# Expert outputs scattered to DRAM rows and gathered by token, in place of a matrix product that combines them

## The reference

```python
grp_p = softmax(t @ router_grp + router_grp_b)        # 4 groups, the best one is taken
exp_logits = (t @ router_exp + router_exp_b)          # 8 experts in that group, the top 2 are taken
# weights w1, w2 of the two experts of each token
y[token] = w1 * expert(e1, t[token]) + w2 * expert(e2, t[token])
expert(e, t) = (silu(t @ w_gate[e]) * (t @ w_up[e])) @ w_down[e]   # 1024 -> 256 -> 1024
x = x + gate * y
out = rmsnorm(x, final_norm_g)
```

## Time and profile before

| | |
|---|---|
| median of 3 runs | 2294.93 us (2294.24 to 2294.96) |
| the profiled execution: its own time, its span | 2294.58 us, 2292.7 us |
| loop over the experts (first L2770 to the last L2868) | 1982.66 to 2273.8 us |
| from there to the end of the span | 18.9 us |
| PE busy over the span | 2112.8 us, 92% |
| mean of the DMA engines in 1993 to 2240 us | 0.87 busy, 360 GB/s |

### The profile page before, as it was taken

The page is one execution under the profiler, slowest core; times in us unless marked ns, Lnnn a source line. Parts: engine busy times, 40 slices in busy tenths (PEclk is TensorE's granted clock), DMA queues, the critical chain, the costliest instruction groups (busy, mean ns, idle before and its releaser), DMA issues. The chain is left out here.

```text
span 2292.7 us, 36330 instructions
## 1 busy us (share of the span) xinstructions
PE 2112.8 (92%) x15874; PEld 1296.2 (57%) x15874; DVE 798.8 (35%) x1625; ACT 512.7 (22%) x1042; POOL 101.1 (4%) x103
## 2 busy tenths in 40 slices
PE   6989999999999999999998887899988997799996
PEld 3545568854445658864544776885488643333332
DVE  1474323211185323310245446436344413311112
ACT  2223322201114413210121332123331201211111
POOL 0000000000000000000000011000012000000000
PEclk9999999999999999999998988899999998899998
DMA  6351325533343236334211000100110163298881
GB/s 260 146 201 56 145 110 220 221 147 147 127 187 139 104 124 257 147 147 155 92 43 51 3 3 2 48 13 37 74 40 3 45 258 131 97 391 349 351 347 59
DMA packets 30507, 313.87 MB, mean 137 GB/s; under 512 B 4744, under 2 KB 7184, under 8 KB 9488
## 3 DMA queue, kind: packets, MB, share of 16 engines
q1 hardware_dynamic: 28048, 308.40, 34.3%
q0 software_dynamic: 2304, 3.15, 0.4%
HBM read 330.39 MB, written 3.16 MB: 145 GB/s over the span
## 5 line engine op out<-in xcount | busy, mean ns | idle before, releaser
L511 ACT ACTIVATE arena<-pair 128x512 f32<-128x512 f32 (+5 forms) x339 | 181.0, 547 | 698.7 <-PE pair L885 170.6
L1262 PE MATMUL pair<-arena,weight_ring 128*128 128x256 f32 x1408 | 310.5, 383 | 2.9 <-ACT arena L785 2.9
L885 PE MATMUL pair<-weight_ring,arena 128*128 128x512 f32 (+1 forms) x640 | 277.0, 586 | 19.1 <-issue 11.3
L1262 PEld LDWEIGHTS pair<-arena,weight_ring 128*128 128x128 f32 x1408 | 269.7, 192 | 43.7 <-issue 6.8
L885 PEld LDWEIGHTS pair<-weight_ring,arena 128*128 128x128 f32 x640 | 122.9, 195 | 155.6 <-issue 150.1
L1308 PE MATMUL pair<-weight_ring,arena 128*128 128x512 f32 x352 | 151.5, 592 | 3.1 <-DVE arena L1282 3.1
L1282 DVE SCALAR_TENSOR_TENSOR arena<-pair,columns,arena 128x255 f32<-128x255 f32 (+1 forms) x176 | 76.7, 477 | 201.8 <-ACT arena L1273 200.3
L1308 PEld LDWEIGHTS pair<-weight_ring,arena 128*128 128x128 f32 x352 | 66.8, 190 | 86.7 <-issue 83.2
L1568 PEld LDWEIGHTS pair<-arena 64*64 64x64 f32 x3584 | 111.9, 140 | 4.4 <-issue 3.7
L1568 PE MATMUL pair<-arena 64*64 64x64 f32 x3584 | 113.8, 224 | 0.0
L1382 PE MATMUL pair<-weight_ring,arena 128*128 128x512 f32 (+1 forms) x256 | 106.5, 574 | 4.5 <-DVE arena L704 4.5
(11 more groups left out here) (473 smaller groups left out, 2642.1 us busy)
## 6 DMA issues: line engine op xcount, KB each, us to landing
weight_ring<-stream SPq DMA_DIRECT2D x85, 2048.0 KB, 7.4
weight_ring<-experts_in SPq DMA_DIRECT2D x17, 2048.0 KB, 10.3
arena<-experts_in SPq DMA_DIRECT2D x15, 2048.0 KB, 11.6
arena<-experts_out SPq DMA_DIRECT2D x8, 2048.0 KB, 14.3
weight_ring<-experts_out SPq DMA_DIRECT2D x8, 2048.0 KB, 13.2
weight_ring<-stream SPq DMA_DIRECT2D x4, 1024.0 KB, 4.8
arena<-rows_in SPq DMA_DIRECT2D x1, 3264.0 KB, 21.8
weight_ring<-stream SPq DMA_DIRECT2D x2, 1152.0 KB, 5.1
```

The lines of the kernel that those rows point to most:

```text
L511: copy_act = lambda dst, src: nc.scalar.activation(dst, src, ACT_F.Copy)
L885: last = mm(bank[b][:, 0:n], hT[:, k, m * P:(m + 1) * P], w[:, k * n:k * n + n], start=(j == 0), stop=(j == KD - 1))
L1262: last = mm(bank[b][:, j * S:(j + 1) * S], w[:, at:at + P], hT[:, k, :], start=(k == 0), stop=(k == KD - 1))
```

## The change

The sorted outputs of the experts are written to a DRAM tensor `y_dram` with a row of 4 KB for each of the 512 places and 16 spare rows. For each pair GpSimd issues one indirect store of `Y`'s 128 rows, 64 for each expert of the pair. A row past the end of its expert goes to a spare row if it is in one of the first 16 partitions, and is left out otherwise. After the last pair four indirect loads fetch, for each of the two halves of the tokens and each of their two choices, 128 rows of 4 KB, and DVE adds them to `x` with their weight. `combine`, `combine_weights`, `posT`, `wT` and their spreading go. `Y` is now scaled by the gate row as DVE reads it from PSUM (both halves on DVE), and the outputs' banks alternate between 2, 3 and 4, 5. The last norm is done for each half of the tokens by itself, with two stores, and the table for the root is loaded ahead. The overflow pairs stand at positions 5, 9, 13 and 17.

```diff
-            for at, w in ((3, 32), (8, 34), (13, 36), (18, 38)):
+            for at, w in ((5, 32), (9, 34), (13, 36), (17, 38)):
...
-            for b, values, out_ in ((0, slots2, posT), (1, w12, wT)):
-                take(b)
...
-            spread_done = c.act
+            def sorted_rows():
+
+                link(tt(picked, taken_by, by_slot(ends), ALU.mult))
+                link(nc.vector.tensor_reduce(limits[:, N_EXP:N_EXP + 8], picked, AX, ALU.add))
+                nc.vector.tensor_copy(limits[:, 0:N_EXP], ends)
+                nc.vector.tensor_scalar(row_at[0:CH], firsts[0:CH, 0:40:2], k3c("slot", 1)[0:CH], None, ALU.add)
+                nc.vector.tensor_scalar(row_spare, k3c("slot", 1), k3c("skip", 1), 2.0 * S, ALU.subtract, ALU.add)
+                link(nc.vector.tensor_scalar(row_at[CH:P], firsts[CH:P, 1:40:2], k3c("slot", 1)[CH:P], -float(CH),
+                                             ALU.add, ALU.add))
+                tt(row_ok[0:CH], row_at[0:CH], limits[0:CH, 0:40:2], ALU.is_lt)
+                link(tt(row_ok[CH:P], row_at[CH:P], limits[CH:P, 1:40:2], ALU.is_lt))
+                link(nc.vector.scalar_tensor_tensor(row_at, row_at, row_spare, row_ok, ALU.subtract, ALU.mult))
+                link(nc.vector.tensor_scalar(row_at, row_at, row_spare, None, ALU.add))
+                nc.vector.tensor_copy(places_i[:, 0:20], row_at)
+                return nc.vector.tensor_copy(places_i[:, 20:24], place2.rearrange("p c m -> p (c m)"))
+            places_mark = dve_after(sorted_rows, ("dve", c.dve))
...
-            def combine_weights(i):
...
             def expert_outputs(i):
-                hT, Y = hTs[i % 2], Ys[i % 2]
+                hT, Y, ob = hTs[i % 2], Ys[i % 2], 2 + 2 * (i % 2)
...
-                    if i >= 1:
-                        PE.wait_ge(act_done, left_done[i - 1])
-                        PE.wait_ge(dve_done, right_done[i - 1])
+                    if i >= 2:
+                        PE.wait_ge(dve_done, rows_done[i - 2])
...
-                    nc.scalar.activation(Y[:, 0, :], bank[2][:, :], ACT_F.Copy).then_inc(act_done, 1)
...
-                    nc.vector.tensor_copy(Y[:, 1, :], bank[3][:, :]).then_inc(dve_done, 1)
+                        DVE.wait_ge(y_sent, 16 * (i - 1))
+                    for h_ in range(2):
+                        last = tt(Y[:, h_, :], bank[ob + h_][:, :], grow[:, 1, 512 * h_:512 * h_ + 512], ALU.mult)
...
-            def combine(i):
...
+            def rows_out(i):
+
+                at = pair_windows[i] // 2
+                if POOL:
+                    POOL.wait_ge(dve_done, rows_done[i])
+                    if i:
+                        POOL.wait_ge(y_sent, 16 * i)
+                    POOL.indirect_dma_start(out=y_dram, out_offset=bass.IndirectOffsetOnAxis(ap=places_i[:, at:at + 1], axis=0),
+                                            in_=Ys[i % 2].rearrange("p a b -> p (a b)"), in_offset=None,
+                                            bounds_check=2 * S + 15, oob_is_err=False).then_inc(y_sent, 16)
...
+            for i in range(npairs + 1):
                 if i < npairs:
                     expert_inputs(i)
                 if 1 <= i < npairs - 1:
                     open_window(i + 1)
                 if 1 <= i <= npairs:
                     hidden(i - 1)
-                if i >= 2:
-                    combine(i - 2)
-                if i < npairs:
-                    combine_weights(i)
                 if 1 <= i <= npairs:
                     expert_outputs(i - 1)
+                    rows_out(i - 1)
...
+            if POOL:
+                POOL.wait_ge(act_done, window_copied[npairs - 1])
+                POOL.wait_ge(dve_done, places_mark[1])
+                POOL.wait_ge(y_sent, 16 * npairs)
+                for m in range(TT):
+                    for q in range(2):
+                        POOL.indirect_dma_start(
+                            out=back[2 * m + q], out_offset=None, in_=y_dram,
+                            in_offset=bass.IndirectOffsetOnAxis(ap=places_i[:, 20 + 2 * q + m:21 + 2 * q + m], axis=0),
+                            bounds_check=2 * S - 1, oob_is_err=False).then_inc(y_back[2 * m + q], 16)
+
+            root_ready = act_after(lambda: nc.scalar.activation(ss[:, 32:33], ss[:, 32:33], ACT_F.Sqrt), ("act", c.act))
+            def last_rows(m):
...
+                def add_experts():
+                    for q in range(2):
+                        if DVE:
+                            DVE.wait_ge(y_back[2 * m + q], 16)
+                        last = nc.vector.scalar_tensor_tensor(x[:, m, :], back[2 * m + q], w12[:, q, m:m + 1], x[:, m, :],
+                                                              ALU.mult, ALU.add)
...
+            together([last_rows(m) for m in range(TT)], [])
```

More of the change, by code:

```diff
@@ L240, in build @@
         stored = sem("stores_done")
+        y_sent = sem("sorted_rows_out")
+        y_back = [sem(f"sorted_rows_back{i}") for i in range(4)]
         spilled = sem("u_spilled")
@@ L2895, in program @@
-            norm_rows(x[:, :, :], xn, TT)
-            for m in range(TT):
-                dve_step(lambda: tt(xn[:, m, :], xn[:, m, :], tail("fin", D), ALU.mult))
+                    rows_out(i - 1)
+            back = [sorted_x.rearrange("p a b -> p (a b)")[:, D * q:D * q + D] for q in range(4)]
+            if POOL:
[8 more added lines that the diff above has]
+                            bounds_check=2 * S - 1, oob_is_err=False).then_inc(y_back[2 * m + q], 16)
@@ new lines, in program, with squares, scaled @@
+            root_ready = act_after(lambda: nc.scalar.activation(ss[:, 32:33], ss[:, 32:33], ACT_F.Sqrt), ("act", c.act))
+            def last_rows(m):
+                s1 = ss[:, m:m + 1]
+                def add_experts():
[4 more added lines that the diff above has]
+                                                              ALU.mult, ALU.add)
+                        if q == 0:
+                            link(last)
+                    return last
+                m_x = dve_after(add_experts)
+                yield
+                def squares():
+                    link(nc.scalar.activation(xn[:, m, :], x[:, m, :], ACT_F.Square, accum_out=s1))
+                    return copy_act(xn[:, m, 0:1], xn[:, m, 0:1])
+                a = act_after(squares, m_x, root_ready)
+                yield
+                d = dve_after(lambda: nc.vector.tensor_scalar(s1, s1, 1.0 / D, EPS, ALU.mult, ALU.add), a)
+                a = act_after(lambda: nc.scalar.activation(s1, s1, ACT_F.Sqrt), d)
+                yield
+                def scaled():
+                    link(nc.vector.reciprocal(s1, s1))
+                    return nc.vector.scalar_tensor_tensor(xn[:, m, :], x[:, m, :], s1, tail("fin", D), ALU.mult, ALU.mult)
+                d = dve_after(scaled, a)
+                if SP:
+                    SP.wait_ge(done[d[0]], d[1])
+                    SP.dma_start(out.rearrange("b (m p) d -> p (b m) d", p=P)[:, m, :], xn[:, m, :]).then_inc(stored, 16)
+                yield
```

68 lines of the change are left out of this document (11 added, 57 removed).

## The result

19 runs of the changed kernel have a median of 2303.34 us (2293.35 to 2313.81), 19 runs of the kernel before on the same chip 2295.79 us. The ratio is 1.0037, with a 95% interval of 1.0025 to 1.0048: slower by 0.37%, 8.5 us (the two medians are 7.6 us apart), where 7.7 us less were forecast. The profiled execution took 2301.17 us with a span of 2299.2, against 2294.58 and 2292.7. The lines of the code have moved: inputs L2777 (before L2770), transposes L2804, copy L2812, outputs L2829, scalings L2841, scatter L2853, gather L2876, additions L2890.

What follows compares the result with a forecast made beforehand. PE bound the kernel, loads close behind and setting the pace after the change. Start and loop 2.7, last pair 4.6 and end 0.4 us saved gave a span of 2285.0, forecast 2287.2 us; own range 2281 to 2291, 8-in-10 range 2276 to 2301.

Steps and rivals of the forecast that it cites:

- the first wait: At pair 3, now plain: five loads must land first, at 2017.9 us, so PE waits 4.9 us.
- the end: After the last scalings: last scatter, four gathers, additions, norm and stores, 22.3 us against 22.7 before.
- The rival of slow trips at the end: Scatter and gather at the end each take 7.5 us, 6.2 us more; chance 0.23 jointly with costlier scatters in the loop.
- From pair 3 to pair 19: 16 loop steps: four overflow pairs at 24.9 us per two steps, eight other steps at 15.27 us, from 2017.9 to 2239.7.
- signs of being wrong: Waitless step far from 11.4 us, plain steps over 16, PE clock under 0.9 in the loop, or end over 26.
- Double step, 24.9: From the start of the pair before an overflow pair to that of the pair behind: 24.9 us, against 28.5 before.
- Plain step, 14.77 without scatter: In runs of plain pairs three 2 MB loads at 426 GB/s set the step: 14.77 us, plus the scatter's share.
- The scatter's share, 0.5 us: Each indirect store in the loop adds 0.5 us to a plain step; bounds 0 and 2 us.
- overflow loads at nothing: The small overflow loads fit in the dry stretch of the load queue around an overflow pair, at no cost.
- The clock: PE's clock drops after waits of about 4 us in the loop; one drop of 3.5 us counted, bounds 0 and 21.
- The rival, which needed four and a half drops to decide: Clock drops before each overflow pair and in the first and last pairs: six, 17.5 us more, 2304.7 us; chance 0.2.
- The rival of uneven scatter: Scatter rows on few DMA engines add 2 us to loads, 12 us over 8 steps; chance 0.23 jointly with slow end trips.

Runs made afterwards that it cites:

- e5: The changed kernel run again, unaltered; ratio 1.0041 to the kernel before.
- e13: The changed kernel with only the last pair's scatter, one row in place of 16 in overflow loads and at most one spare row; ratio 0.9997 to the kernel before.
- e1: The changed kernel with two idle products before the inputs of each plain pair from pair 3 on; 2310.90 us, ratio 1.0053 to the kernel before.
- e6: The changed kernel with the 16 rows of an overflow load spread over every fourth partition; ratio 1.0026 to the kernel before.
- e9: The changed kernel with four slots for input weights and three for output weights, input loads first; 2286.13 us, ratio 0.9954 to the kernel before.
- e11: The kernel before with only the slots dealt out anew, four for input and three for output weights; ratio 1.0008 to the kernel before.
- e10: The changed kernel with four input and three output slots, one row in overflow loads and at most one spare row; 2274.52 us, ratio 0.9885 to the kernel before.
- e8: The changed kernel with all 128 rows of every scatter written, unused ones to spare rows; ratio 1.0095 to the kernel before.

## Why the prediction was wrong

Right were: that the loads take over from PE; PE's step (11.43 for 11.37); the start (1981.56 for 1981.65); the first wait (2018.4 for 2017.9); the last pair (12.2 for 12.5); the end (23.3 for 22.3, its two DRAM trips included); no wait at an overflow pair. The rival of slow trips at the end falls: the scatter landed after 2.6 us, the gathers after 4.2 to 6.2. Scatters took 966 to 1218 ns of POOL, but none of the 20 ran while VectorE was busy. Eight other indirect DMAs did, seven overflow loads and a gather, for 0.07 to 0.96 us each, and took 987 to 1001 ns, no more than the others of their kind (993 to 1039). So nothing is to be seen here of the lock in the Trainium skill, "SBUF — State Buffer", section "A bandwidth-pool intuition that's wrong (but worth ruling out)"; its example is a copy on VectorE, and here VectorE ran `tensor_tensor` and `scalar_tensor_tensor`.

**The step that failed is "From pair 3 to pair 19".** 221.8 us were forecast for it, plus 3.5 for the clock; the two profiles have 238.3 and 232.8, so 13.0 and 7.5 us more, and that is the whole miss: with 0.5 at the start, -0.3 in the last pair and 1.0 at the end, 13.0 makes the 14.2 by which the span is over its forecast of 2285.0. In the second profile (e5) the span is 2304.0: there the loop also starts 9.4 us later than forecast, which is no effect of the change, since nothing ahead of it is altered and the four profiles of the kernel before and its variants start it between 1982.5 and 1990.1 as well. Of the signs of being wrong that the prediction names, one came: the mean plain step of the first profile is 16.06 us. By terms:

- *Double step, 24.9.* Even with neither scatter nor overflow rows it is 26.0 where no drop falls into it (e13: 26.2, 25.5, 26.3). 1.1 us times four: 4.5 us. The 2.9 us ahead of a transfer, read from two loads with nothing more behind them, are 4.3 to PE's start with further loads behind the awaited one.
- *Plain step, 14.77 without scatter.* It is 15.0 in e13: 2 us in eight.
- *The scatter's share, 0.5 us, and overflow loads at nothing.* Plain steps take 120.3 us in e13, 126.0 and 128.5 with both: 5.7 to 8.2 us in place of 4. By the timed ratios the two cost 9 to 10 us (e13 against the changed kernel). My reason for nothing, that they "fit in the dry stretch", is refuted by the timeline of POOL: they are issued into the end of a load that PE awaits. Their cost was asked of the wrong stretch, the mean of the queue over 393 us, where it had to be asked of the few us ahead of each wait.
- *The clock.* One drop of 3.5 us was taken; 2.8 us in one profile, 6.7 in the other. The term, 3.5, lies between them, though one drop cost 1.7 to 2.9 us and not 3.5 and it took three of them to make 6.7. The rival, which needed four and a half drops to decide, fell. That drops in plain pairs cost nothing agrees with e1.

The rival of uneven scatter had the right place for part of the miss and the wrong reason for most. Spreading the overflow rows more than halved the landing of the input rows, and the kernel gained nothing that is told apart from noise (0.15%). By the Trainium skill, "DMA: Bandwidth & Descriptors", section "The descriptor swizzle", partitions 0 to 15 are served by engines 0 to 3; by its rule the 16 rows of an overflow load lie on four engines in e5 and one on each of 16 in e6. The 8.3 and 3.5 us agree with that in direction.

The terms make 4.5 + 2.1 + 1.7 - 0.7 = 7.6 for the second profile (7.5 measured) and 4.5 + 2.1 + 4.2 + 3.2 = 14.0 for the first (13.0). They say why no gain came, and don't prove each tenth: the two executions differ by 5.5 us in the loop.

**Where the gain went.** PE's step got 2.84 us shorter (14.27 to 11.43), 57 us over 20 steps; the loads let through none of it. That isn't bandwidth alone: at 0.83 the DMA engines are idle a sixth of the stretch. Around an overflow pair no slot is free for the next pair until PE has finished the inputs ahead, and of the three loads that then start the ring puts one input load last, behind output weights that PE needs only a step later. PE starts a load's time later than it could, and with it all that frees the next slots. That order was free while PE's 28.5 us covered it. e9 turned it round with the same bytes, and 20 us came out; e11, with no gain in the kernel before, shows that it takes the shorter PE step and the new order together.

**Open** stay the shares of scatter and overflow rows (they don't add), what the 7 us of the scatter beyond its bytes are, and how much of the loss is the move of the overflow pairs, 0.24% in the kernel before and not separable in the changed one.

## What to carry to other kernels

Where two resources are within a few per cent of each other, taking work from the one gives only the difference; what comes next is decided by the order in which buffers come free, so walk the slots and ask at each dry stretch of the queue which slot it waits for. Small transfers are not free in "idle" time unless their issue falls into it: read the issue times beside the landing that is awaited. And a latency read from loads with nothing behind them is too short for one with others behind it. Last, let the load that is needed first go first: the order in which a ring of slots hands them out may say otherwise.

## What the runs showed of the hardware

- An indirect load of 16 rows of 16 KB landed after 8.3 us (median, e5) with its rows on neighbouring partitions and after 3.5 (e6) with them spread, beside the same stream of large loads.
- PE's granted clock fell to 0.50, the lower of its two levels (1.2 of 2.4 GHz), after waits as short as 2.2 us (e10, pair 19: a wait of 2.18 us, then inputs of 8.8 us in place of 7.05; pair 4: 2.29 and 8.78), but stayed at 1.00 after one of 3.76 us in e9 (pair 19), and after one of 3 us in the earlier trace rows. The length of the last wait alone doesn't decide it.
- 8 MB more of scattered rows of 4 KB cost 12 us (6 to 19 by the intervals) beside 86 MB of loads (e8 against e5); at 426 GB/s they take 19 us. That part of them goes into stretches in which the queue is dry is not shown.
- A load of 2 MB behind which nothing is queued landed 3.0 us later than the transfers of the queue add up to (two loads); with further loads behind it, 4.0 us later (e13, second and third load of three).
